# Scaling each head's exponentials by a per-row scalar, one operation per token tile, in a four-layer two-model transformer kernel

## The reference

```python
def global_gqa(q, k, v):              # first model, 8 heads
    ...
        s = jnp.einsum('bqkgd,bskd->bkgqs', qblk, k).astype(jnp.float32) * scale
        p = jax.nn.softmax(s, axis=-1).astype(v.dtype)
        return jnp.einsum('bkgqs,bskd->bqkgd', p, v)

def dilated_window_attention(q, k, v): # first model, 8 heads
    ...
            p = jnp.exp(s - lse).astype(v.dtype)
            outs.append(jnp.einsum('bhqj,bqjhd->bqhd', p, vg).astype(jnp.float32))

def dsa_attention(q, k, v, q_idx, k_idx, w_idx):   # second model, 6 heads
    ...
        p = jax.nn.softmax(s, axis=-1)
        return jnp.einsum('bqhk,bqkd->bqhd', p, vg).astype(q.dtype)

def diff_attention(q, k, v, lam, g_sub, lam_init): # second model, 4 heads
    ...
        p = jax.nn.softmax(jnp.where(causal, s, -jnp.inf), axis=-1)
        a = p[:, :, 0] - lam * p[:, :, 1]

def moba_attention(q, k, v):                       # second model, 6 heads
    ...
            p_own = jax.nn.softmax(s_own, axis=-1)
            return jnp.einsum('bhqk,bhkd->bhqd', p_own, v_own)
```

## Time and profile before

| what | value |
|---|---|
| median of the runs shown | 1909.38 us (three runs, 1909.2 to 1916.82) |
| span of the profiled execution, first to last instruction | 1912.1 us |
| mean granted TensorE clock in it | 0.983 of full speed |
| PE busy | 95% of the span |
| DVE busy | 74% |
| ACT busy | 59% |
| POOL busy | 21% |
| L1290, all 56 | 52.7 us on DVE, 942 ns mean |

### The profile page before, as it was taken

The page is one execution under the profiler, slowest core; times in us unless marked ns, Lnnn a source line. Parts: engine busy times, 40 slices in busy tenths (PEclk is TensorE's granted clock), DMA queues, the critical chain, the costliest instruction groups (busy, mean ns, idle before and its releaser), DMA issues.

```text
span 1912.1 us, 26024 instructions
## 1 busy us (share of the span) xinstructions
PE 1824.1 (95%) x8799; PEld 1486.2 (78%) x8799; DVE 1416.6 (74%) x1631; ACT 1122.6 (59%) x1296; POOL 392.8 (21%) x315
## 2 busy tenths in 40 slices
PE   7899999989999998899989879999999999999997
PEld 6678886868888786688878667888888888888885
DVE  5748874466976586644458758889888888888897
ACT  6745444564443464443345537777777777777775
POOL 3722203463212363200046500000000000000000
PEclk9999999999999999999999989999999999999999
DMA  8348884418987341455544258999999999999994
GB/s 271 111 161 327 343 342 147 149 54 323 344 347 275 91 152 45 154 195 179 192 154 142 69 187 334 386 376 386 380 384 376 383 383 381 380 374 381 381 387 167
DMA packets 237934, 506.45 MB, mean 265 GB/s; under 512 B 23304, under 2 KB 74720, under 8 KB 231712
## 3 DMA queue, kind: packets, MB, share of 16 engines
q1 hardware_dynamic: 225664, 492.91, 70.9%
q0 software_dynamic: 3008, 10.32, 2.0%
q10 hardware_dynamic: 9184, 2.23, 0.5%
HBM read 497.49 MB, written 7.91 MB: 264 GB/s over the span
## 4 chain that ended last, share of the span: by engine, by line
PE 83%; DVE 7%; issue 6%; ACT 3%; POOL 1%; DMA 0%; POOLq 0%; SPq 0%; DVEq 0%; ACTq 0%
PE bank L2351 25%; PE bank L2353 25%; PE bank L2352 25%; PE bank L2470 2%; ACT slab L2042 1%; PE bank L2789 1%; DVE slab L1290 1%; PE bank L2561 1%; PE bank L2539 1%; ACT w_hi L1892 1%; PE bank L2521 1%; POOL w_lo L826 1%; DVE x L1074 0%; PE bank L2572 0%; DVE slab L1271 0%
## 5 line engine op out<-in xcount | busy, mean ns | idle before, releaser
L977 DVE TENSOR_TENSOR w_lo<-slab,w_hi 128x2048 fp32r<-128x2048 f32 x369 | 847.8, 2308 | 214.3 <-ACT w_hi L1892 213.3
L1892 ACT ACTIVATE w_hi<-slab 128x2048 fp32r<-128x2048 f32 (+2 forms) x421 | 796.6, 1898 | 329.0 <-PE bank L2353 256.3
L2351 PE MATMUL bank<-w_hi,hT_hi 128*128 128x512 f32 (+3 forms) x1664 | 649.4, 390 | 14.2 <-DVE hT_lo L1012 4.4
L2352 PE MATMUL bank<-w_lo,hT_hi 128*128 128x512 f32 (+3 forms) x1664 | 638.0, 383 | 0.0
L2353 PE MATMUL bank<-w_hi,hT_lo 128*128 128x512 f32 (+3 forms) x1664 | 637.9, 383 | 0.0
L2351 PEld LDWEIGHTS bank<-w_hi,hT_hi 128*128 128x128 f32 x1664 | 316.0, 190 | 77.9 <-DVE w_lo L977 8.8
L2353 PEld LDWEIGHTS bank<-w_hi,hT_lo 128*128 128x128 f32 x1664 | 315.5, 190 | 59.7
L2352 PEld LDWEIGHTS bank<-w_lo,hT_hi 128*128 128x128 f32 x1664 | 316.3, 190 | 55.3
L826 POOL TENSOR_TENSOR w_lo<-slab,w_hi 128x512 fp32r<-128x512 f32 (+2 forms) x208 | 262.4, 1295 | 381.3 <-ACT w_hi L1892 361.6
L2351 PE MATMUL bank<-w_hi,hid_hi 128*128 128x512 f32 x680 | 265.6, 391 | 0.7 <-DVE w_lo L977 0.7
L2353 PE MATMUL bank<-w_hi,hid_lo 128*128 128x512 f32 x680 | 265.0, 390 | 0.0
(11 more groups left out here) (252 smaller groups left out, 1232.0 us busy)
## 6 DMA issues: line engine op xcount, KB each, us to landing
slab<-in_w_exp_gate SPq DMA_DIRECT2D x176, 512.0 KB, 7.0
slab<-in_w_exp_up SPq DMA_DIRECT2D x176, 512.0 KB, 7.5
slab<-in_w_exp_down SPq DMA_DIRECT2D x176, 512.0 KB, 7.1
slab<-in_w_ada SPq DMA_DIRECT2D x48, 1024.0 KB, 5.5
slab<-in_w_mlp_in SPq DMA_DIRECT2D x64, 512.0 KB, 5.4
slab<-in_w_mlp_out SPq DMA_DIRECT2D x64, 512.0 KB, 9.0
slab<-in_w_in SPq DMA_DIRECT2D x56, 512.0 KB, 5.0
slab<-in_w_out SPq DMA_DIRECT2D x32, 512.0 KB, 4.6
```

What stands on the lines that cost most here:

```text
L977: dve.tensor_tensor(w_lo[:, q, 0:n], raw(s)[:, 0:n], w_hi[:, q, 0:n].bitcast(F32), ALU.subtract).then_inc(lo_dve, 1)
L1892: act.activation(w_hi[:, q, 0:n], raw(s)[:, 0:n], ACT.Copy).then_inc(hi_done, 1)
L2351: pe.matmul(dst, a_hi, b_hi, start=start, stop=False)
L2352: pe.matmul(dst, a_hi, b_lo, start=False, stop=False)
```

## The change

For each head of the branch, the one product of a 128 x 512 tile with a reciprocal broadcast over 256 keys becomes two products, one for each token tile of 128 x 256, with the reciprocal as a scalar for each row. Each counts `nrm_done` by 1, so that PE's waits see the same sum when both are done. All else is the same on all engines.

```diff
                         for s, p in enumerate((p0, p1)):
                             dve.wait_ge(ex_done, 4 * (U0 + u) + 2 * s + 2)
                             link(dve.reciprocal(r[:, s, :], att[:, 2, 2 * u + s, :]))
-                            dve.tensor_tensor(p, p, r[:, s, :].unsqueeze(2).broadcast_to([P, TT, SEQ]), ALU.mult).then_inc(nrm_done, 2)
+                            for t in range(TT):
+                                dve.tensor_scalar(p[:, t], p[:, t], r[:, s, t:t + 1], None, ALU.mult).then_inc(nrm_done, 1)
```

## The result

| what | before | after |
|---|---|---|
| median of the runs | 1911.67 us (four runs, 1909.2 to 1916.82) | 1923.12 us (four runs, 1921.69 to 1924.83) |
| span of the profiled execution | 1912.1 us | 1919.9 us (its time is 1921.74) |
| mean granted clock in it | 0.983 | 0.984 |

The ratio of the times is 1.0062, with a 95% interval of 1.0049 to 1.0076: slower, by some 9 to 15 us.

What follows compares the result with a forecast made beforehand. PE bounds most of the span, but DVE, excluded by POOL, sets the pace in some attention stages. Layers 0 and 1 add 9.4 us, layers 2 and 3 3.6: +13.0 on 1909.4 gives 1922.4 us, range 1907 to 1928.

Steps and rivals of the forecast that it cites:

- The mechanism: Heads beside a busy POOL: POOL, already waiting, goes first between the halves, so the second half waits a full POOL operation.
- the forecast's path: Layers 0 and 1: DVE's lateness reaches unit 5's maxima, ACT's exponentials and PE's sums of squares, 4.7 us for each layer.
- Rival (a): Halves stay together ahead of POOL; each head gains 0.07 us, time 1908 us; chance 0.15.
- (c): A half fits POOL's gap, under 0.24 us; second heads' waits on the chain vanish, -8 us, below 1900; chance 0.05.
- (b): POOL goes between in only part of the heads, or ACT and PE absorb part: 1914 to 1918 us; chance 0.15.
- One sign: The new line at 77 to 95 us: first halves of 0.35 to 0.45 us, second halves near 1.4, POOL operations between.
- The price of a half: Each 128 x 256 scalar product on DVE: 348 ns, from the trace's 128 and 512 element sizes.
- The 0.97 us for a head: Each head beside a busy POOL goes from W + 0.69 to W + 1.66 us, W being the first POOL wait.
- Layers 0 and 1: Units 2 and 3 each 1.94 us late, unit 4 0.9; 4.8 at unit 5's maxima, +4.7 a layer, +9.4 together.
- Layers 2 and 3: Unit 4 about 0, units 5 to 7 gain some 0.15 us, unit 8 loses 1.94: +1.8 a layer, +3.6 together.
- The clock: PE's 1.2 GHz spells after the DVE stage, left out of the sum: longer PE waits could add 0 to +3 us.

Runs made afterwards that it cites:

- experiment 2: Kernel before, with scalar halves only in the units that have no POOL work beside them, one product elsewhere; 1915.7 us, ratio 1.0019 to before.
- 1 to 6 and 8: Against before: two-operand halves 1.0093; halves where POOL idles 1.0019, works 1.0088; row-sum halves 0.9953; POOL cut 0.994, 0.9932; one product a unit 1.0031; row sums only beside POOL 0.994.
- experiment 1: Kernel before, each head's product split into two halves of the old two-operand form, without the scalar form; 1930.47 us, ratio 1.0093 to before.
- experiment 7: Changed kernel, with POOL's tiles in eight operations of 256 columns in place of four of 512; 1913.03 us, ratio 1.001 to before.

## Why the prediction was right

**The mechanism** came out as it stood. POOL goes between the halves in every head beside which it still has operations; the forecast's path, DVE to the next maxima, ACT's exponentials and PE's sums of squares, is the chain of the changed kernel. POOL's 16 operations end at 94.44 us (forecast near 94); the last 12 of them fall 3, 2, 3, 2 and 2 in and between units 2 to 4, as the forecast counted. Rival (a), halves that stay together, falls with the timeline; (c), halves that fit POOL's gap, falls too, since every second half beside POOL waits out a whole operation; and (b) would need heads beside POOL that pay nothing or a part, of which units 2 and 3 have none. One sign was put wrongly: first halves of 0.35 to 0.45 us came only in first heads. In second heads they took 1.16 to 1.17, the wait W for POOL's first operation, which the sum had and the sign forgot.

**The price of a half** was forecast as 348 ns from two other sizes of that operation; the median is 354, and 351 (345 to 356) in the 56 halves of experiment 2, which have no POOL operation beside them. The 194 ns of the Trainium skill (VectorE: DVE Perf Modes, the errata section) is not reached by any of the 112.

**The 0.97 us for a head** was a little too large. Unit 2 takes 1.76 us more, 0.88 for each head; unit 3 (85.09 to 89.53, before 82.26 to 84.94) likewise, unit 4 0.74 where 0.9 was forecast. Of the 0.09 too much, 0.07 is a gain that the sum did not know: the old product began 0.11 us after the reciprocal that it waits for had ended (77.81 to 77.92), the half 0.03 after (78.89 to 78.92). The rest is that a second half ends 1.27 us after the first instead of 1.31, less 0.02 by which W grew.

**Layers 0 and 1** were forecast at 4.7 us each and gave 3.96 and 3.93. The units beside POOL gave 4.3 of the 4.8; the free heads of unit 1 ahead of them gave back about 0.3, which the forecast left out. **Layers 2 and 3** were forecast at 1.8 each and gave 1.57 and 1.54: unit 4 gave nothing, as forecast, unit 8 gave 1.74 where 1.94 was forecast, units 5 to 7 gave back 0.4 where it was 0.15, and 0.2 came in ahead of the stage. The sum is 11.0 instead of 13.0, beside 11.5 between the medians. That the median came out within 1 us of the 1922.4 forecast is partly luck: the forecast stood on a median of before of 1909.38, which with a fourth run became 1911.67.

**The clock** was left out with 0 to +3 us. In the profiled pair the spells cost 1.6 us in layer 2 and gave back 1.6 in layer 0 and 3.1 at the experts; over all runs the medians differ by 9 to 15 us, so against the 11.0 of DVE's stages it leaves -2 to +4. The experiments hint that it isn't nothing: in 1 to 6 and 8 the medians differ from before by 2 to 6 us more than DVE's stages do, always to the same side (+19.0 against +16.4 in experiment 1; -12.3 against -9.6 in the kernel before without POOL). Whether the clock carries this was not tested.

## What to carry over

Before an operation is split, look at what an engine that excludes it does in that stretch, and whether that engine is already waiting: each cut is one more place where it can go first, and the price is as a rule the other's whole operation, not the fixed cost of one's own (0.88 us a head here, for halves of 0.35). Look also for a form of the same operation that isn't excluded at all; it may be longer by itself and still win (0.48 us instead of 0.35, and 0.5% faster than before instead of 0.6% slower). And an early or late start moves what is met further on: an edit in untroubled units can lose in the troubled ones.

## What the hardware showed that was not expected

- The scalar operation that also writes out its row sum neither waits for POOL nor delays it: 473 to 481 ns in all 112, beside POOL operations of 1.26 to 1.27 us in layer 0.
- A half starts 0.03 us after the end of the reciprocal that it waits for, the product of a whole head 0.10 to 0.11. It isn't the scalar form: the two-operand halves of experiment 1, with their broadcast reciprocal, start as early. What makes the difference stays open.
- One DVE operation of 128 x 2 took 13.68 us, through 21 POOL operations of 0.58 to 0.73 in a row (experiment 7); up to the end of layer 3's attention no other DVE operation in any trace took over 1.2 us more than the shortest of its line and form.
- Where a product meets POOL's operation decides its time: begun 0.13 us after POOL's start it took 1.68 us, begun 0.19 ahead of its end 0.74.
- Spells at 1.2 GHz moved between kernels that do the same work in a stretch: the same 98 matmuls took 26.15 us at a granted clock of 0.82 and 23.04 at 0.94.
